# Sums of squares in the mixers: two fp32r products of split squares instead of one fp32 product

## The reference

```python
h = h + 0.5 * rmsnorm(swiglu(rmsnorm(h, g), w_gate, w_up, w_down), g2)      # FFN 1
u = rmsnorm(h, mix_pre_g)
z, xbc, dt_raw, q, k, v, gate_logits = split(u @ w_in)
y_ssd = ssd_branch(z, xbc, dt_raw, ...)       # 4 groups; ends in an rmsnorm over each group's 512 features
y_att = diff_attn_branch(q, k, v, ...)        # 8 heads; each head's 128 outputs go through an rmsnorm
h = h + rmsnorm((gate0 * y_ssd + gate1 * y_att) @ w_out, mix_post_g)
h = h + 0.5 * rmsnorm(swiglu(...), ffn2_post_g)                             # FFN 2
# second block
u = rmsnorm_2(h, norm1_g); proj = u @ w_in_2
gq, gk = l2norm(...), l2norm(...)             # 8 heads of a gated delta rule, each q and k normed over 128 features
ik = layernorm_nobias(i_k)                    # the indexer's key
h = h + mixed(gated delta rule, sparse attention with the indexer's top 256 keys) @ w_out_2
h = h + ffn_w_down(silu(conv(gate)) * conv(val));  return rmsnorm_2(h, final_g)
```

## Time and profile before

| | before |
|---|---|
| median of 3 runs | 2519.9 us (2519.49 to 2521.68) |
| the profiled execution, its own time | 2522.89 us |
| its span, first to last instruction | 2521.1 us |
| mean granted PE clock, share of full speed | 0.997 |
| PE matmuls busy | 2485.8 us, 99% |
| PE weight loads busy | 2050.7 us, 81% |
| DVE busy | 1616.6 us, 64% |
| ACT busy | 1202.0 us, 48% |

### The profile page before, as it was taken

One profiled execution on the slowest core, in us unless ns is written; L12 is line 12 of the kernel. 1 busy time (PEld: TensorE's weight loads), 2 busy tenths in 40 slices (PEclk: granted clock), 3 DMA queues, 4 the chain that ended last, 5 costly groups with the idle time before them and its releaser, 6 DMA issues.

```text
span 2521.1 us, 37085 instructions
## 1 busy us (share of the span) xinstructions
PE 2485.8 (99%) x15074; PEld 2050.7 (81%) x15074; DVE 1616.6 (64%) x2555; ACT 1202.0 (48%) x1997; POOL 76.1 (3%) x114
## 2 busy tenths in 40 slices
PE   9999999999999999999999999999999999999998
PEld 7999878887877777878999878777776788888887
DVE  6888338866765545248888257766877645677733
ACT  6555334766556455246555236544333454444421
POOL 0111000000000000000110000000000000000000
PEclk9999999999999999999999999999999999999999
DMA  5776332222222222233775323211111112233232
GB/s 166 178 180 157 109 100 84 76 83 76 76 67 76 76 68 76 92 93 96 175 180 153 96 92 100 70 43 39 46 43 51 59 53 91 94 99 100 88 100 72
DMA packets 80523, 237.79 MB, mean 94 GB/s; under 512 B 8928, under 2 KB 10976, under 8 KB 80352
## 3 DMA queue, kind: packets, MB, share of 16 engines
q1 hardware_dynamic: 68832, 213.56, 26.8%
q0 software_dynamic: 10080, 18.35, 4.8%
q10 hardware_dynamic: 1440, 3.49, 0.4%
HBM read 233.27 MB, written 2.10 MB: 93 GB/s over the span
## 4 chain that ended last, share of the span: by engine, by line
PE 90%; DVE 5%; DMA 2%; ACT 1%; issue 1%; POOL 0%; SPq 0%; ACTq 0%; DVEq 0%
PE bank L2088 22%; PE bank L2090 21%; PE bank L2089 21%; PE bank L2102 4%; PE bank L2104 3%; PE bank L2103 3%; PE bank L2332 2%; PE bank L2257 1%; PE bank L2171 1%; DMA raw<-in_w1u 1%; PE bank L2265 1%; PE bank L2251 1%; PE bank L2428 1%; PE bank L2238 1%; DVE hl L2827 1%
## 5 line engine op out<-in xcount | busy, mean ns | idle before, releaser
L2088 PE MATMUL bank<-uR,hl 128*128 128x512 f32 x1696 | 690.7, 407 | 3.7 <-DVE uR L2844 3.1
L2833 DVE TENSOR_TENSOR hl<-raw,hl 128x1024 fp32r<-128x1024 f32 (+2 forms) x325 | 386.0, 1191 | 476.3 <-ACT hl L2477 474.9
L2090 PE MATMUL bank<-uR,hl 128*128 128x512 f32 x1696 | 663.1, 391 | 0.0
L2089 PE MATMUL bank<-uR,hl 128*128 128x512 f32 x1696 | 662.3, 391 | 0.0
L2477 ACT CAST hl<-raw 128x1024 fp32r<-128x1024 f32 (+2 forms) x325 | 329.9, 1020 | 218.6 <-PE bank L2090 211.9
L2088 PEld LDWEIGHTS bank<-uR,hl 128*128 128x128 f32 x1696 | 319.4, 188 | 95.0 <-issue 25.3
L2089 PEld LDWEIGHTS bank<-uR,hl 128*128 128x128 f32 x1696 | 319.6, 188 | 68.5 <-issue 7.7
L2090 PEld LDWEIGHTS bank<-uR,hl 128*128 128x128 f32 x1696 | 318.9, 188 | 68.6
L2827 DVE TENSOR_TENSOR hl<-raw,hl 128x1024 fp32r<-128x1024 f32 (+1 forms) x142 | 150.7, 1075 | 29.3 <-ACT hl L2473 25.7
L2102 PE MATMUL bank<-sum,hl 128*128 128x256 f32 x560 | 159.1, 284 | 2.5 <-DVE fA L2979 2.4
L2103 PE MATMUL bank<-sum,hl 128*128 128x256 f32 x560 | 158.4, 283 | 0.0
(11 more groups left out here) (491 smaller groups left out, 4191.2 us busy)
## 6 DMA issues: line engine op xcount, KB each, us to landing
raw<-in_win SPq DMA_DIRECT2D x147, 512.0 KB, 3.5
raw<-in_w SPq DMA_DIRECT2D x44, 512.0 KB, 3.5
raw<-in_w1u SPq DMA_DIRECT2D x54, 256.0 KB, 3.1
raw<-in_w2u SPq DMA_DIRECT2D x51, 256.0 KB, 3.3
raw<-in_w1g SPq DMA_DIRECT2D x22, 512.0 KB, 4.6
raw<-in_w2g SPq DMA_DIRECT2D x22, 512.0 KB, 4.5
raw<-in_w1d SPq DMA_DIRECT2D x16, 512.0 KB, 3.5
raw<-in_wssd SPq DMA_DIRECT2D x16, 512.0 KB, 3.5
```

The costliest lines, as they stand in the source:

```text
L2088: e.matmul(s.bank[:, :], h[:, 0, w], hi, start=s.first and q == 0, stop=False)
L2089: e.matmul(s.bank[:, :], h[:, 0, w], lo, start=False, stop=False)
L2090: i = e.matmul(s.bank[:, :], h[:, 1, w], hi, start=False, stop=s.last and q == n - 1)
L2833: e.tensor_tensor(h[:, 1, w], x[:, w], h[:, 0, w].bitcast(F), ALU.subtract).then_inc(*sig("dve_split.lo", s, i))
```

## The change

In the mixers the squared tile is split like everything else: `sq_split` lets ACT copy it to an fp32r tile `hi` and DVE subtract that to get `lo`. `rstd_split` then multiplies both with the ones, read as fp32r, into one bank. The four tiles for `hi` and `lo` (`sqR`, the pool `sp`) lie in SBUF where `raw` has T1 to T4S. So the FFNs' sums wait until the mixer is done with them (`free`, `t_sq`), and the mixers' squares until the FFN is done (`t_phase`). Two waits are new in the main stream: `room(4)` ahead of each projection of an attention head, and one for a pair of pages in `kp` ahead of v of the delta rule.

```diff
@@ costs
+    if k == "rstd_split":
+        return [("PE", 0.47, "pe_norm.sum"), ("ACT Ln", 0.7, "act_norm.ln"), ("ACT Exp", 0.63, "act_norm.r")]
+    if k == "sq_split":
+        return [("ACT", 0.62), ("DVE", 0.69, "dve_norm.sq_lo")]
@@ build
-    raw = sb(ctx, "raw", [128, 2 * NRAW + 4, 512])
+    with ExitStack() as ph:
+        raw = sb(ph, "raw", [128, 2 * NRAW + 4, 512])
+    sb(ctx, "raw_slots", [128, 2 * NRAW, 512])
+    sqR = sb(ctx, "sqR", [128, 4, 512], R)
...
-    def side_rstd(src, which):
-        yield from ready(*[t for x, t in src])
-        qs = [fp.take() for _ in src]
-        s = step("squares", src=src, qs=qs)
-        t = [("act_norm.sq", s, i) for i in range(len(src))]
-        yield from ready(t, banks=1)
-        r = rstd([(q[:, :], [t[i]]) for i, q in enumerate(qs)], which)
-        for q in qs:
-            q.release(("pe_norm.sum", r.s))
+    def rstd_split(q, which):
+        yield from until(lambda: len(sp.left) > 1)
+        hi, lo = sp.take(), sp.take()
+        s = step("sq_split", q=q, hi=hi, lo=lo, ready=list(q.t))
+        q.release(("dve_norm.sq_lo", s))
+        yield from ready(("dve_norm.sq_lo", s), banks=1)
+        b, r = SB.take(), fp.take()
+        r.s = s = step("rstd_split", hi=hi, lo=lo, of=s, which=which, b=b, r=r)
+        b.release(("act_norm.ln", s))
+        for x in (hi, lo):
+            x.release(("pe_norm.sum", s))
+        r.t = [("act_norm.r", s)]
         return r
+
+    def side_rstd(x, which):
+        yield from ready(x)
+        q = fp.take()
+        s = step("squares", src=[(x[:, :], list(x.t))], qs=[q])
+        q.t = [("act_norm.sq", s, 0)]
+        yield from ready(q)
+        return (yield from rstd_split(q, which))
@@ group_rstd
-        yield from ready(("dve_norm.sum4", s2, 2), banks=1)
-        r = rstd([(qs[0][:, :], [("dve_norm.sum4", s2, 2)])], which)
-        qs[0].release(("pe_norm.sum", r.s))
-        return r
+        yield from ready(("dve_norm.sum4", s2, 2))
+        qs[0].t = [("dve_norm.sum4", s2, 2)]
+        return (yield from rstd_split(qs[0], which))
@@ ffn: load_pair, second_sum, fourth_sum
-                         T3: sum_by_dma(t3, f"t3_{j % 2}", wu[j][:, 0:512], wu[j][:, 512:1024], list(t3_free[j % 2]))}
+                         T3: sum_by_dma(t3, f"t3_{j % 2}", wu[j][:, 0:512], wu[j][:, 512:1024], free + t3_free[j % 2])}
-                ts[j][T2] = step("tsum_2", b1=rs[j][0], t3=T1 + j % 2, landed=[rs[j][1], ts[j][T3]])
+                ts[j][T2] = step("tsum_2", b1=rs[j][0], t3=T1 + j % 2, landed=[rs[j][1], ts[j][T3], *free])
-                ts[j][T4S] = step("tsum_4", b1=rs[j][0], s=ts[j][T2])
+                ts[j][T4S] = step("tsum_4", b1=rs[j][0], s=ts[j][T2], after=free)
@@ project_head
         for name, j in (("q", 40 + h), ("k", 48 + h), ("v", 56 + h)):
+            yield from room(4)
             b = yield from ugemm(WIN[j])
@@ project_gdn
+        yield from until(lambda: "v2" in S[h - h % 2] or kp.left)
         b = yield from ugemm(W2[16 + h])
@@ around FFN 2
+    t_sq = [x for _, after in sp.left for x in after]
-    ys, b7, b_sum = ffn(G2, U2, d["w2d"], "ffn2_post", "ffn2_pre", 2, t_all, FIRST2)
+    ys, b7, b_sum = ffn(G2, U2, d["w2d"], "ffn2_post", "ffn2_pre", 2, t_all + t_sq, FIRST2)
@@ tensor_program
+        def rstd_split(s):
+            go.wait_ge(*on("pool_init.ones", s_init, s.which))
+            after(*s.b.after)
+            go.wait_ge(*on("dve_norm.sq_lo", s.of))
+            one = onesc[:, s.which, :].bitcast(R)
+            e.matmul(s.b[:, :], one, s.hi[:, :], start=True, stop=False)
+            e.matmul(s.b[:, :], one, s.lo[:, :], start=False, stop=True).then_inc(*sig("pe_norm.sum", s))
@@ ACT's and DVE's programs
+        def sq_split(s):
+            after(*s.ready, *s.hi.after)
+            e.copy(s.hi[:, :], s.q[:, :]).then_inc(*sig("act_norm.sq_hi", s))
+        def sq_split(s):
+            go.wait_ge(*on("act_norm.sq_hi", s))
+            after(*s.lo.after)
+            e.tensor_tensor(s.lo[:, :], s.q[:, :], s.hi[:, :].bitcast(F), ALU.subtract).then_inc(*sig("dve_norm.sq_lo", s))
```

More of the change, by code:

```diff
@@ L278, in build @@
     fp = Pages(low, "fA")
+    sp = Pages([], "square pages")
     act, con, mR, fB = [None] * 3, [None] * 2, [None] * 2, [None] * 2
@@ L1128, in build @@
     fp.left += [(fB[0][:, i, :], t_phase) for i in range(NB1)]
+    sp.left = [(sqR[:, i, :], t_phase) for i in range(4)]
     rp = Pages([mR[0][:, i, :] for i in range(16)], "R pages")
@@ L1474, in att_head @@
         V.release(tpv)
-        r = yield from side_rstd([(o[:, :], o.t)], O128)
+        r = yield from side_rstd(o, O128)
         yield from ready(r)
@@ L1637, in l2 @@
     def l2(x, scale, to=None, half=0):
-        r = yield from side_rstd([(x[:, :], x.t)], O1)
+        r = yield from side_rstd(x, O1)
         yield from ready(r)
@@ L1909, in index_side @@
         b.release(*x.t)
-        r = yield from side_rstd([(x[:, :], x.t)], O128)
+        r = yield from side_rstd(x, O128)
         yield from ready(r)
@@ L2428, in sp_front @@
             e.matmul(s.b[:, 0:W], s.q[:, tcol(s.i)], s.k[:, 0:W], start=True, stop=True).then_inc(*sig("pe_spa.S", s))
-        do = {"mm": mm, "product": product, "lead": lead, "sum_first": sum_first, "keep": keep, "mm_half": mm_half, "end_first": end_first, "end_sum": end_sum, "rstd": rstd, "decay_turn": decay_turn, "ssd_x": ssd_x, "ssd_cb": ssd_cb,
+        do = {"mm": mm, "product": product, "lead": lead, "sum_first": sum_first, "keep": keep, "mm_half": mm_half, "end_first": end_first, "end_sum": end_sum, "rstd": rstd, "rstd_split": rstd_split, "decay_turn": decay_turn, "ssd_x": ssd_x, "ssd_cb": ssd_cb,
               "ssd_state": ssd_state, "ssd_front": ssd_front, "ssd_from": ssd_from, "ssd_y": ssd_y, "turn_v": turn_v,
@@ L2786, in scalar_program @@
         do = {"init": init, "act_split": act_split, "fast_hi": fast_hi, "fast_x": fast_x, "fast_copy": fast_copy, "fast_silu": fast_silu,
-              "con": con_load, "split": split, "fold": fold, "fold_sq": fold_sq, "end_add": end_add, "end_sum": end_sum, "squares": squares, "rstd": rstd, "warm": warm,
+              "con": con_load, "split": split, "fold": fold, "fold_sq": fold_sq, "end_add": end_add, "end_sum": end_sum, "squares": squares, "rstd": rstd, "rstd_split": rstd, "sq_split": sq_split, "warm": warm,
               "last_sq": last_sq, "post_fold": post_fold, "norm_u": norm_u, "fold_h": fold_h, "ffn_gate": ffn_gate, "ffn_mul": ffn_hi, "collect": collect,
@@ L2974, in tsum_4 @@
             go.wait_ge(*on("dve_fast.t", s.s))
+            after(*s.after)
             e.tensor_tensor(raw[:, T4S, :], raw[:, s.b1 + 1, :], raw[:, T2, :], ALU.add).then_inc(*sig("dve_fast.t", s))
@@ L3481, in vector_program @@
         do = {"setup": setup, "ids": ids, "act_split": act_split, "fast_scale": fast_scale, "fast_sum": fast_sum, "fast_lo": fast_lo,
-              "tsum_2": tsum_2, "tsum_4": tsum_4, "fast_add": fast_add, "fast_mul": fast_mul, "split": split, "scale": scale, "fold": fold, "fold_sq": fold_sq, "end_add": end_add, "end_out": end_out, "post_fold": post_fold, "sq_sum": sq_sum,
+              "tsum_2": tsum_2, "tsum_4": tsum_4, "fast_add": fast_add, "fast_mul": fast_mul, "split": split, "scale": scale, "fold": fold, "fold_sq": fold_sq, "end_add": end_add, "end_out": end_out, "post_fold": post_fold, "sq_sum": sq_sum, "sq_split": sq_split,
               "norm_x": norm_x, "norm_u": norm_u, "fold_h": fold_h,
```

## The result

The changed kernel takes 2536.9 us (median of 5 runs, 2534.4 to 2537.6) against 2519.9 us of the kernel before on the same chip (2518.6 to 2521.8): ratio 1.0064, 95% interval 1.0052 to 1.0075. It is 17.0 us **slower**. The profiled execution took 2536.46 us (before: 2522.89). The forecast was 2516 us in a range of 2508 to 2523, so it missed the side as well as the range.

The account below looks back on a forecast made before the run. PE's instruction queue was taken to set the end, with side chains pacing bare stretches of the second mixer. -11.9 + 4.9 + 1.0 + 2.0 = -4.0 gave 2518.9 us profiled, 2516 for the median; range 2508 to 2523.

Parts of the forecast that it names:

- The price of a sum: PE, 29 mixer sums: two fp32r products take 0.45 us instead of 0.86, winning 11.9 us in all.
- The rival that two products keep two old slots: PE, changed sums: two products still take two slots of 0.43 us; +7.9 us, 2528 us, chance 0.03.
- The guard `room(4)`: First mixer, attention head 0: empty page pool holds the main stream until `ssd_core(1)` ends; +4.9 us idle, bounds 0 and +7.0.
- +1.0 for the clock: After the gaps expected at head 0: lower granted clock slows the next weight matmuls; bounds 0 and 1.2 us.
- Two square pairs at a time instead of four: Second mixer, `l2`: third and fourth norms wait for the first two, claimed to fit inside 3.2 us.
- the 3.2 us: Second mixer, each pair's `l2` phase: lengthening by four more ACT copies and a subtraction, 4 x 0.62 + 0.69.
- the +2.0 us for the second mixer: Second mixer: cost of longer `l2` phases exposing missing weight sums in bare stretches; bounds 0 and 9.6 us.
- a gap of the kind in the earlier trace: Second mixer, bare stretches: each missing weight sum exposes 0.3 us of PE wait (2.6 us in 8 waits); 2.7 us if all missed.
- the side chain that sets the pace of the second mixer: Second mixer: pairs 1 to 3 win nothing and each `l2` phase adds 3.2 us; +8.5, 2528 us, chance 0.10.
- PE stays without idle time in attention: Sign at 940 to 1040 us: PE still has no idle time there after the change.
- the waits for the square tiles: FFN, SP's queue and DVE's `tsum_2`, `tsum_4`: cost nothing; otherwise up to 1 to 2 us once.
- The `kp` guard: Second mixer, ahead of v of the delta rule: binds only if `gdn_turn_k` of the pair before is late.

Follow-up runs that it names:

- The guards alone: Kernel before plus only the two new main-stream waits (`room(4)` and the one for `kp`), every sum one fp32 product: 2528.5 us, ratio 1.0027.
- `l2` in full precision: Changed kernel with the 16 `l2` sums back in one fp32 product, other sums split, both guards kept: 2527.3 us, ratio 1.0027.
- four at once: Changed kernel with `l2` taking its hi and lo tiles from the ten free `gx` pages, so no norm waits for tiles: 2522.9 us, ratio 1.0011.
- k split: Changed kernel with only the two k norms of each pair split, the two q norms in one fp32 product: 2520.7 us, ratio 0.9998.
- `ROOM2 = 5`: Changed kernel with the planner holding the second mixer's main stream at 5 free pages instead of 6: 2529.9 us.

## Why the prediction was wrong

**The price of a sum, 0.41 us each, was right.** Two products 0.23 us apart, and 10.6 us of 11.9 between two kernels that differ in nothing else. The rival that two products keep two old slots is out.

**The guard `room(4)` was right in its place and near in its size.** Forecast were +4.9 us idle and +1.0 for the clock. The guards alone gave 6.4 us in the first mixer. In the changed kernel PE is idle for 4.4 us at 570 to 580, and the clock of 0.50 and 0.67 comes to 2.9 us by the same account as in the second mixer (PE's busy time in the first is 2.0 us shorter, where the slots alone make 4.9). For the first mixer -4.9 + 5.9 = +1.0 was forecast and +2.7 came. Part of that is chance: four versions with the same order there (`l2` in full precision, four at once, k split, `ROOM2 = 5`) show +0.6 or +0.7, with a clock of 0.77 to 0.89 at 575 to 580.

**The step that failed** is "Two square pairs at a time instead of four make the third and fourth `l2` wait for the first two, inside the 3.2 us", and with it the +2.0 us for the second mixer. The 3.2 us were the work that ACT and DVE get more. The wait for a free tile isn't that work: it is a whole trip of cast, subtraction and a place in PE's queue, with the root ahead of the next cast in ACT's order. It measured 7.1 us from the first two casts to the other two in the second pair and 11.2 to the third in the first, and the four sums of a pair were spread over 9 to 14 us instead of 3 to 6. With four pairs of tiles nearly the same work costs 14 us less. The forecast's +2.0 was the second mixer without the slots saved; measured the same way it is 14.7 + 7.0 = 21.7 us.

**What a late preparation exposes was wrong too.** The prediction took "a gap of the kind in the earlier trace rows", 0.3 us each, because that was what most waits there measured. But the main stream was out of pages well before the recurrence started, no weight sum stood there, and PE waited for DVE's steps for 1.6 to 2.3 us. The row to price it by was in the earlier trace rows as well: the one wait of 2.0 us at `L2341`, with the clock of 0.89 in the earlier trace rows beside it. In place of nine gaps of 0.3 us came 9.4 us more of idle time at 1700 to 1900, 3.2 more at 1930 to 2000, and 9.2 us of lower clock. The scans, which the prediction didn't name, have a good part of it (8.9 us of waits against 3.2). Here the Trainium skill has the sign to look for: "Perfetto Trace Analysis", section Optimization Strategy, reads the same bubble coming back on the busy engine as a possible lack of buffers for the next tile. The trace agrees: the same wait at `L2372` in three pairs, 6.2 us.

**The rival that came nearest** is the side chain that sets the pace of the second mixer. It was priced at +9.6 from the chain's own lengthening, at most, and at 2528 us in all. It had the right place and sign; as a bound it was too low (9.6 against 21.7), since it had neither the wait for a tile nor the lower clock (9.2 us) in it. The chance of 0.10 rested on DVE's share of the bare stretches and not on when the main stream is held.

**The rest.** That PE stays without idle time in attention is right (100.00 us busy at 940 to 1040), and FFN 2 and the tail have their length of before within 0.6 us, so the waits for the square tiles there cost nothing. The `kp` guard costs nothing by itself. What stays open is how the 14.7 us divide between the rounds and the place of the holds: no version has the rounds of the changed kernel with the holds of the kernel before. That the two ways around the wait for a tile (four at once, k split) both bring the second mixer back to within 0.7 us of before, with 7.0 and 3.7 us of slots saved, speaks for the rounds. That each also has new holds, and that those alone are worth 6 us, is why it isn't proof of the size.

## What to carry to other kernels

Count what a new step holds and not only what it does: a pool of temporary tiles that is smaller than the number of chains that run side by side turns them into rounds, each as long as the whole trip over all engines. If a planner fixes the order by the free buffers, a late side chain is paid for by the main stream, and its price is the longest bare wait in the profile, with the clock after it, instead of the mean one. The plan says in advance where to look: at the holds that have already lasted some us when the side stream comes to steps with nothing beside them. And before a part of the difference is put down to a cause, move the order without that cause once: here that alone was worth 6 us in a kernel to which nothing had been done.

## What the runs showed of the hardware

In the changed kernel PE waited 2.1 us up to 571.83 and 2.6 us up to 577.35. The products that begin at 573.30, between the two waits, already take 0.43 us for two where the same two took 0.22 at 568.40, and the granted clock over 575 to 580 was 0.50. It was still 0.67 over 580 to 585, though PE was busy all the time, and the pitch of the weight sums is 0.43 us up to 583.26. The same place in four other versions had a clock of 0.77 to 0.89 over 575 to 580: what a gap costs in clock differed from one execution to another. In the second mixer of the changed kernel the lower clock took nearly as much as the added idle time (9.2 against 12.8 us).

A product with full float32 operands takes 0.86 us of PE in two records and two fp32r products of the same size take 0.45, though the weights are loaded in two loads of 188 ns in both cases.
